# The shared expert's product and the router's logits in one, and a new order of the projection's tiles, in an encoder layer

## What is computed

```python
x = ln_affine(DN_ALPHA * x + gate1 * mixer(u, p), p['ln1_g'], p['ln1_b'])
u = ln_plain(x) * (1.0 + scale2) + shift2
# moe(u): router and shared expert
scores = jax.nn.sigmoid((xt @ p['w_router']).astype(jnp.float32))      # 1024 x 64
g, up = jnp.split(xt @ p['w_sh_in'], 2, axis=-1)                       # 1024 x 512
shared = (jax.nn.silu(g) * up) @ p['w_sh_out']                         # 256 x 1024
```

## Time and profile before

| what | us |
|---|---|
| time, median of 3 runs (2921.95 to 2924.55) | 2923.84 |
| the profiled execution's own time | 2924.61 |
| its span | 2922.4 |
| TensorE busy | 2761.5 |
| VectorE busy | 1585.7 |
| ScalarE busy | 691.7 |
| GpSimd busy | 1107.5 |
| the tile loop, from the first projection to the experts' first product | 983.7 to 1477.4 |

### The profile page before, as it was taken

One profiled execution on the slowest core, in us unless ns is written; L12 is line 12 of the kernel. 1 busy time (PEld: TensorE's weight loads), 2 busy tenths in 40 slices (PEclk: granted clock), 3 DMA queues, 4 the chain that ended last, 5 costly groups with the idle time before them and its releaser, 6 DMA issues. The chain is left out here.

```text
span 2922.4 us, 31454 instructions
## 1 busy us (share of the span) xinstructions
PE 2761.5 (94%) x9161; PEld 1327.1 (45%) x9161; DVE 1585.7 (54%) x2552; ACT 691.7 (24%) x1205; POOL 1107.5 (38%) x1150
## 2 busy tenths in 40 slices
PE   6999999899999899899899999999999999999990
PEld 2345445455555355444444444444444444444440
DVE  3477257778877477778734333333333333343436
ACT  2354354366666211111100000000000000000004
POOL 2002001100000123233356656666665666565664
PEclk9999999999999899999899999999999999999995
DMA  8531000300000311221187798986978788899647
GB/s 335 190 113 55 18 33 8 154 20 8 12 12 8 141 50 59 87 80 58 58 276 230 222 324 227 314 254 163 291 211 262 205 233 251 273 289 301 184 100 273
DMA packets 189009, 466.46 MB, mean 160 GB/s; under 512 B 21756, under 2 KB 46526, under 8 KB 187518
## 3 DMA queue, kind: packets, MB, share of 16 engines
q1 hardware_dynamic: 137246, 311.89, 29.7%
q0 software_dynamic: 51680, 153.50, 21.6%
HBM read 361.38 MB, written 99.75 MB: 158 GB/s over the span
## 5 line engine op out<-in xcount | busy, mean ns | idle before, releaser
L1249 PE MATMUL mx_pH<-ring,mx_wsi 128*128 (+1 forms) x2096 | 944.3, 593 | 5.0 <-DVE mx_wsi L1171 3.0
L1103 POOL DMA_INDIRECT kT<-s_u,ex_gidx x532 | 602.9, 1133 | 163.8 <-issue 159.0
L1249 PEld LDWEIGHTS mx_pH<-ring,mx_wsi 128*128 128x128 f32 x2096 | 388.5, 190 | 445.3 <-issue 445.2
L1269 PE MATMUL mx_pU<-qT,mx_hT 128*128 x1040 | 467.5, 592 | 0.0
L1171 DVE STREAM_TRANSPOSE mx_wsi<-kT 128x1024 f32<-128x1024 f32 x132 | 164.0, 1242 | 321.1 <-DMA kT<-s_u,ex_gidx 315.3
L1269 PEld LDWEIGHTS mx_pU<-qT,mx_hT 128*128 128x128 f32 x1040 | 197.6, 190 | 248.7 <-issue 248.7
L1127 POOL DMA_INDIRECT s_acc<-mx_wso,ex_sidx x130 | 211.8, 1629 | 187.6 <-DVE mx_wso L1201 125.2
L1201 DVE SCALAR_TENSOR_TENSOR mx_wso<-mx_pU,mx_wsi 128x1024 f32<-128x1024 f32 x130 | 166.8, 1283 | 191.7 <-PE mx_pU L1269 186.7
L1154 ACT ACTIVATE mx_hT<-mx_pB 128x256 f32<-128x256 f32 x130 | 49.8, 383 | 870.1 <-PE mx_pB L1236 870.1
L1175 DVE TENSOR_TENSOR mx_h<-mx_silu,mx_pH 128x256 f32<-128x256 f32 x131 | 54.9, 419 | 330.4 <-ACT mx_silu L1143 329.7
L638 PE MATMUL fr_pF<-fr_uT,fr_wf 128*128 128x512 f32 x512 | 224.9, 595 | 1.3 <-ACT fr_uT L332 1.3
(11 more groups left out here) (311 smaller groups left out, 3169.0 us busy)
## 6 DMA issues: line engine op xcount, KB each, us to landing
ring<-in_w_exp_in SPq DMA_DIRECT2D x64, 2048.0 KB, 11.9
qT<-in_w_exp_out SPq DMA_DIRECT2D x64, 1024.0 KB, 15.5
fr_wq<-in_w_ada SPq DMA_DIRECT2D x32, 512.0 KB, 4.8
kT<-s_u,ex_gidx POOLq DMA_INDIRECT x536
fr_wf<-in_w_in SPq DMA_DIRECT2D x16, 512.0 KB, 5.6
s_u<-v SPq DMA_DIRECT2D x16, 512.0 KB, 2.7
out_z<-s_acc SPq DMA_DIRECT2D x16, 512.0 KB, 11.9
y<-out_z SPq DMA_DIRECT2D x16, 512.0 KB, 4.6
```

The costliest lines, as they stand in the source:

```text
L1103: nc.gpsimd.indirect_dma_start(xg[:, u, g, :], None, u2_q, bass.IndirectOffsetOnAxis(ap=gidx[:, u, g:g + 1].bitcast(U32), axis=0)).then_in ...
L1249: m = nc.tensor.matmul(pH[:], xT[:, u, k, :], wi[:, bass.ds(slot, 1), k, :].rearrange("p a f -> p (a f)"), start=(k == 0), stop=(k == KD - 1))
L1269: m = nc.tensor.matmul(pY[:, h, :], hT[:, c, :], wo[:, bass.ds(slot, 1), c, h * 512:(h + 1) * 512].rearrange("p a d -> p (a d)"), start=(c ...
```

## The change

Three things. The router's weights lie in the same buffer as the shared expert's first weights, ahead of them, and for tiles 1 to 12 the first matmul takes 320 columns (64 logits and 256 for silu) into pH and a second one the other 256 into pB. TensorE's order in a tile becomes: attention half 0, turn, attention half 1, product of 320, product of 256, lru half 0 of the next tile, `gated`, lru half 1 of the next tile, `shared_out`, `rank`. On VectorE the gate stands between the second statistics and their aggregation, and the adding of the shared output goes from `norms(i-1)` to the head of tile i; SyncE stores z and loads x accordingly. New waits: the product of 256 waits for the gate before (h_ready) and for the slots two tiles back, `gated` also for the scores (ez_ready), `rank` also for the gate.

```diff
-        wr, wsi, wso = sb("mx_wr", [P, KD, N_EXP]), sb("mx_wsi", [P, KD, 2 * D_E]), ...
+        wsi, wso = sb("mx_wsi", [P, KD, 2 * D_E + N_EXP]), sb("mx_wso", [P, NB, D_E // P, D])
-        LOG, RNK = 0, 64
+        UP, LOG, RNK = 0, D_E, D_E + N_EXP
+        FIRST = N_EXP + D_E
 # SyncE, tile i
-                if 0 < i <= LATE:
-                    store_z(i - 1)
+                if 2 <= i <= LATE + 1:
+                    store_z(i - 2)
+                if i >= 2 and i + 1 < NT:
+                    load_x(i + 1)
                 sp.wait_ge(u2_ready, i + 1)
...
-                if i and i + 2 < NT:
-                    load_x(i + 2)
 # ScalarE
-                if i > 1:
-                    act.wait_ge(log_mm, i - 1)
+                if 1 < i <= LATE + 1:
+                    act.wait_ge(up_mm, i - 1)
+                elif i > 1:
+                    act.wait_ge(log_mm, i - 1 - LATE)
...
+                scores(i, pB[:, LOG:LOG + N_EXP])
+                if i <= LATE:
                     gated_rows(i)
-                scores(i, pB[:, LOG:LOG + N_EXP])
 # VectorE: in stats, in norms, in gate, in the loop
                 passed(dve, apart)
+                if amid is not None:
+                    gate(amid)
...
-                stats(z, 1, EPS, V2, var2)
+                stats(z, 1, EPS, V2, var2, i - 1 if 0 < i <= LATE else None)
...
-                if 0 < i <= LATE:
-                    add_shared(i - 1)
                 dve.wait_ge(rstd2, i + 1)
...
+                up = bank_of(i + 1)[:, D_E:2 * D_E]
+                if i < LATE:
+                    dve.wait_ge(up_mm, i + 1)
+                    up = pB[:, UP:UP + D_E]
...
             for i in range(NT):
+                if 1 < i <= LATE + 1:
+                    add_shared(i - 2)
                 add_lru(i)
...
-                if 0 < i <= LATE:
-                    gate(i - 1)
                 add_att(i)
 # TensorE
+            def lru_half(i, h):
+                if i and h == 0:
+                    pe.wait_ge(l_added, i)
+                if i == KT and h == 0:
+                    pe.wait_ge(wo_folded, GQ)
+                m = project(pL, 1, lruT, i, h)
+                if h:
+                    m.then_inc(pl_mm, 1)
...
+                if i <= LATE:
+                    for k in range(KD):
+                        m = nc.tensor.matmul(pH[:, 0:FIRST], uT(i, k), wsi[:, k, 0:FIRST], start=(k == 0), stop=(k == KD - 1))
+                    m.then_inc(h_mm, 1)
+
+                    if i > 1:
+                        pe.wait_ge(h_ready, i - 1)
+                    if i > 2:
+                        pe.wait_ge(slots_ready, i - 2)
+                    for k in range(KD):
+                        m = nc.tensor.matmul(pB[:, UP:UP + D_E], uT(i, k), wsi[:, k, FIRST:], start=(k == 0), stop=(k == KD - 1))
+                    m.then_inc(up_mm, 1)
+                    return
...
                 pe.wait_ge(m_ready, i)
                 pe.wait_ge(ez_ready, read)
+                pe.wait_ge(h_ready, min(read, LATE))
...
                 project(pA, 0, attT, i, 0)
+                if i:
+                    turn(i)
+                project(pA, 0, attT, i, 1).then_inc(pa_mm, 1)
                 if i:
                     pe.wait_ge(ut_copied, i)
                 if 0 < i <= LATE:
                     shared_in(i)
-                project(pA, 0, attT, i, 1).then_inc(pa_mm, 1)
+                    lru_half(i + 1, 0)
+                    gated(i)
+                    lru_half(i + 1, 1)
+                    shared_out(i)
...
                 if i >= 2:
                     rank(i - 1, i)
+                if (i == 0 or i > LATE) and i + 1 < NT:
+                    lru_half(i + 1, 0)
+                    lru_half(i + 1, 1)
```

More of the change, by code:

```diff
@@ L1294, in mixing @@
         sem = lambda n: ctx.enter_context(nc.semaphore("mx_" + n))
-        wr, wsi, wso = sb("mx_wr", [P, KD, N_EXP]), sb("mx_wsi", [P, KD, 2 * D_E]), sb("mx_wso", [P, NB, D_E // P, D])
+        wsi, wso = sb("mx_wsi", [P, KD, 2 * D_E + N_EXP]), sb("mx_wso", [P, NB, D_E // P, D])
         rb, ln, iota, tokf = sb("mx_rb", [P, N_EXP]), sb("mx_ln", [P, 2, D]), sb("mx_iota", [P, N_EXP]), sb("mx_tokf", [P, 1])
@@ L1358, in mixing @@
             [sem("u2_stored0"), sem("u2_stored1")])
-        ut_mm, ut_copied, h_mm, silu_ready, h_ready, ht_mm, ht_copied = (sem("ut_mm"), sem("ut_copied"), sem("h_mm"), sem("silu_ready"), sem("h_ready"),
+        up_mm, ut_mm, ut_copied, h_mm, silu_ready, h_ready, ht_mm, ht_copied = (sem("up_mm"), sem("ut_mm"), sem("ut_copied"), sem("h_mm"), sem("silu_ready"), sem("h_ready"),
                                                                         sem("ht_mm"), sem("ht_copied"))
@@ L1393, in _ @@
             load_x(1)
-            sp.dma_start(wsi[:], w_sh_in.rearrange("(k p) f -> p k f", p=P)).then_inc(w_in, 16)
+            sp.dma_start(wsi[:, :, N_EXP:], w_sh_in.rearrange("(k p) f -> p k f", p=P)).then_inc(w_in, 16)
             gate2 = lambda b: mod_d[b:b + 1, 5 * D:6 * D].partition_broadcast(P)
@@ L1398, in _ @@
             sp.dma_start(g2[:], gate2(0)).then_inc(g2_in, 16)
-            for dst, src in ((wr[:], w_router), (rb[:], router_bias.partition_broadcast(P)), (iota[:], iota_d.partition_broadcast(P))):
+            for dst, src in ((wsi[:, :, 0:N_EXP], w_router), (rb[:], router_bias.partition_broadcast(P)), (iota[:], iota_d.partition_broadcast(P))):
                 sp.dma_start(dst, src).then_inc(r_in, 16)
@@ L1504, in silu @@
                     act.wait_ge(h_ready, i - 1)
-                nc.scalar.activation(silu_of(i), bank_of(i)[:, 0:D_E], ACT.Silu).then_inc(silu_ready, 1)
+                nc.scalar.activation(silu_of(i), bank_of(i)[:, N_EXP:FIRST] if i <= LATE else bank_of(i)[:, 0:D_E], ACT.Silu).then_inc(silu_ready, 1)
             def gated_rows(i):
@@ L1513, in scores @@
             def scores(i, logits):
-                act.wait_ge(log_mm, i)
+                if i <= LATE:
+                    act.wait_ge(h_mm, i)
+                    logits = pH[:, 0:N_EXP]
+                else:
+                    act.wait_ge(log_mm, i - LATE)
                 if i > 2:
@@ L1577, in fold, with stats @@
                 nc.vector.scalar_tensor_tensor(wo[:, w, j, :], stg[:, c % 2, :], cg[:, w, j:j + 1], grow[:], ALU.mult, ALU.mult).then_inc(wo_folded, 1)
-            def stats(z, which, eps, var_col, done):
+            def stats(z, which, eps, var_col, done, amid=None):
                 for c in range(2):
@@ L1607, in gate @@
                 dve.wait_ge(silu_ready, i + 1)
-                nc.vector.tensor_tensor(gated_of(i + 1), silu_of(i + 1), bank_of(i + 1)[:, D_E:2 * D_E], ALU.mult).then_inc(h_ready, 1)
+                up = bank_of(i + 1)[:, D_E:2 * D_E]
+                if i < LATE:
+                    dve.wait_ge(up_mm, i + 1)
+                    up = pB[:, UP:UP + D_E]
+                nc.vector.tensor_tensor(gated_of(i + 1), silu_of(i + 1), up, ALU.mult).then_inc(h_ready, 1)
             def router(i):
@@ L1764, in shared_in @@
                     pe.wait_ge(r_in, 48)
+                if i <= LATE:
+                    for k in range(KD):
[9 more added lines that the diff above has]
+                    return
                 for k in range(k0, k1):
-                    m = nc.tensor.matmul(bank_of(i), uT(i, k), wsi[:, k, :], start=(k == 0), stop=(k == KD - 1))
+                    m = nc.tensor.matmul(bank_of(i), uT(i, k), wsi[:, k, N_EXP:], start=(k == 0), stop=(k == KD - 1))
                 if k1 == KD:
@@ L1771, in gated @@
                 pe.wait_ge(h_ready, i)
+                if i <= LATE:
+                    pe.wait_ge(ez_ready, i)
                 for c in range(FC):
@@ L1777, in logits @@
                 for k in range(KD):
-                    m = nc.tensor.matmul(out, uT(i, k), wr[:, k, :], start=(k == 0), stop=(k == KD - 1))
+                    m = nc.tensor.matmul(out, uT(i, k), wsi[:, k, 0:N_EXP], start=(k == 0), stop=(k == KD - 1))
                 m.then_inc(log_mm, 1)
@@ L1805, in block_experts @@
                 nc.tensor.transpose(pB[0:2, LOG:LOG + P], wk[:, 0:2], ident).then_inc(blocks_mm, 1)
+            lru_half(0, 0)
+            lru_half(0, 1)
             for i in range(NT):
                 if i:
[L1809 to L1815, removed]
                     pe.wait_ge(a_added, i)
@@ L1823, in _ @@
                     shared_in(i)
-                project(pA, 0, attT, i, 1).then_inc(pa_mm, 1)
-                if 0 < i <= LATE:
+                    lru_half(i + 1, 0)
                     gated(i)
[L1827 to L1831, removed]
+                    lru_half(i + 1, 1)
+                    shared_out(i)
+                elif i:
+                    if i == LATE + 1:
+                        pe.wait_ge(h_ready, LATE)
+                    pe.wait_ge(ez_ready, i - 1)
+                    pe.wait_ge(slots_ready, i - 2)
                     logits(i, pB[:, LOG:LOG + N_EXP])
-                if 0 < i <= LATE:
-                    shared_out(i)
```

(3 more changed lines are left out.)

## The result

| | before | after |
|---|---|---|
| time, median, us | 2923.77 (2921.95 to 2924.55) | 3016.7 (3015.53 to 3017.7) |
| span of the profiled execution, us | 2922.4 | 3014.3 |
| TensorE busy, us | 2761.5 | 2774.1 |
| start of turn 1, 2, 3, us | 1011.76, 1041.30, 1068.66 | 1012.85, 1038.93, 1073.66 |
| start of turn 13 and 16, us | 1355.62, 1422.92 | 1452.15, 1515.93 |

The ratio is 1.0319, with a 95% interval of 1.0304 to 1.0333: 93 us slower. The loss lies between turn 2 and turn 13: 1355.62 - 1041.30 = 314.3 us before, 1452.15 - 1038.93 = 413.2 after, 98.9 more. Outside it the changed kernel gains 3.5 us from turn 1 to 2 and 3.5 from turn 13 to 16, and begins 1.1 later.

What follows compares the result with a forecast made beforehand. Ordinary tiles were taken as bound by TensorE without waits; the change would close a ring of 35.1 us plus 2.6 of clock per step, adding 94.3 us to 2923.84: 3018 us, 8 in 10 between 2992 and 3038.

Steps and rivals of the forecast that it cites:

- The products: TensorE's 320- and 256-column products take 4.31 and 3.45 us, so its work falls by 0.83 us in each of 12 tiles.
- Rival 2: The ring closes and narrow products do not hide weight loads, 3.5 us per tile: 3057, or 3033 us; chance 0.07.
- The ring: Turn (eight transposes of u), TensorE's tile through rank sums, `ranks`, `router`, `add_shared`, next turn: a closed chain of 35.1 us.
- the answers: Two semaphore responses between TensorE and VectorE within each step, put at 0.2 us in sum.
- The stall: TensorE idles 8.6 us per step just before the turn, until VectorE's `add_shared` releases it.
- Which wait is last: The turn waits last for `add_shared`, queued behind `ranks`, which waits for the rank sums; other chains are not later.
- Rival 3: VectorE reaches `add_shared` early enough, the ring stays open and TensorE remains the bound at 26.53 us: 2911 us; chance 0.05.
- rival 4: The ring opens in some tiles, so about half the steps are long: about 2965 us; chance 0.06.
- The clock: TensorE's clock falls after each stall before the turn, costing 2.6 us per step, between 1.6 and 3.5.
- the granted clock that I named as a sign: In the profile after, granted clock would be near 0.93 in the stretches from turn to turn, tiles 3 to 12.
- Rival 1: The ring closes but TensorE's clock does not fall, or returns at once: 2995 us; chance 0.12.
- Tile 7 and the ends: Step with weight folds 41.5 us; turn 1 to 2 26.1; turn 13 to 16, paced by VectorE, 63.4.

Runs made afterwards that it cites:

- the filler: Changed kernel with attention half 0 computed three times over ahead of the turn, tiles 3 to 13: 2991.74 us.
- the run with both cuts: Changed kernel with rank sums behind attention half 1 and the addition of the shared output between `ranks` and `router`: 2909.72 us.
- the run with more in the ring: Changed kernel plus two VectorE statistics instructions between `router` and the addition, tiles 2 to 12: 3026.53 us; between norms and `ranks` instead: 3016.61 us.
- the first two experiments: Changed kernel, either with VectorE's addition put ahead of `ranks`: 2932.16 us; or with TensorE's rank sums moved just behind attention half 1: 2929.44 us.

## Why the prediction was right, step by step

- **The products**: computed 4.31 and 3.45 us from a line through the rows of 128 and 512 columns; measured 4.31 and 3.45. At 256 columns an instruction costs 3.45 / 16 = 0.216 us, so its weight load stays hidden. Rival 2 is out.
- **The ring**: computed 35.1 us; 34.73 at the one step at full clock before the turn that ends it, 35.05 with the filler. Its pieces, computed and measured: from the turn to the rank sums' end 23.25 and 23.14 (turn 2, at full clock); `ranks` and `router` 10.41 and 10.42 (1136.70 to 1147.12); the addition 1.22 and 1.22; the answers 0.2 in sum, measured 0.03 and 0.10. The stall was set at 8.6 and is 8.3.
- **Which wait is last**: shown by cutting the ring at each joint (2932 and 2929 us) and by the same two instructions inside and beside it (3026.5 and 3016.6). Rival 3 was what the changed kernel would be without the ring; the run with both cuts gives 2909.7, where rival 3 had 2911. No step from turn 3 to turn 13 is below 37.3 us, so rival 4, a ring open in some tiles, is out too. VectorE's 21 us per tile were as before all along; its busy share said nothing of the order.
- **The clock**: 2.6 us per step was taken; measured are 37.45 - 35.05 = 2.4 in the tile shown, and 2.3 to 2.8 over the nine ordinary steps. The rows of the instructions give the same: 1.74 - 0.87 for the turn and 5.06 - 3.44 for the half, 2.5 us. The value held, the way to it only in part. I took granted clock below full, times the length of the stretch, as loss. In the changed kernel that gives 0.14 x 37.45 = 5.2 us, twice the real loss, because the clock also stands low while TensorE waits, where it costs nothing: granted clock is 0.69 over the 8.33 us of waiting (1140.15 to 1148.48), which is 2.6 of the 5.2. In the two stretches around tile 7 of the kernel before, the same product came near the truth: TensorE's busy time there is 3.6 and 1.9 us above the ordinary 27.36, against 3.5 and 1.6 by the product. For the same reason the granted clock that I named as a sign, near 0.93, was 0.86. That stalls of 8.3 us would cost what stalls of up to 4.6 us had cost was assumed, not shown; the run with more in the ring has costs from 1.4 to 3.0 us after stalls of one length. So the nearness of 2.6 is partly luck. Rival 1 is out.
- **Tile 7 and the ends**: the fold's step was put at 41.5 us and is 40.34; turn 13 to 16 was 63.4 and is 63.8; turn 1 to 2 26.1 and 26.08. Turn 16 comes 93.0 us later than before, against 94.3 predicted.

The measured 3016.7 lies 1.3 us below the 3018 predicted. The pieces were off by about as much each, and partly cancel: turn 1 came 1.1 us later than taken and turn 2 to 3 was 0.4 shorter, the nine ordinary steps were 1.2 shorter in sum, the fold's step 1.2 shorter, and turn 13 to 16 0.4 longer.

## What to carry to other kernels

Sum up the work of each engine, but then follow every buffer from its reader to its next writer through all queues: an instruction that frees a buffer must not stand behind a wait for the writer's own last work. Where such a ring is closed, its length is the step, whatever the busy shares; it opens by moving either the release ahead of the wait or the awaited work earlier in its queue, and best so that both have something to spare. A saving on the bound engine shows only as far as the next chain has slack. In the old order VectorE's way to the next turn had 0.7 us to spare, and the matmuls taken away, 1.73 us of logits, were part of what covered it: nothing was gained. With both joints opened an ordinary step is 0.8 us shorter, and turn 1 to turn 16 takes 397.6 us instead of 411.2, which includes about 3 us in the first step, most of it clock, and 3 in the last three.

## What the runs showed of the hardware that was not expected

- Added matmuls made the kernel faster: 6.9 us more of them per tile in a wait of 8.3 us brought 25 us in all, since the clock did not fall. (The prediction does not speak of it; the expectation of that run did.)
- The time at the low level after a stall is not the same for each, not even after stalls of one length: after 8.33 us of waiting the turn and the half behind it took 6.85 us, after 9.66 us of waiting 5.71, and after 9.70 us 7.31, against 4.31 at full clock.
- Waits of 1.6 to 1.9 us in the ordinary tiles, as in the first two experiments, left the granted clock at 1.00. In the first of them one wait of 2.12 us was followed by 1.7 us of loss, and one of 2.50 us, in tile 7, by none (the lru half behind it is 3.60 us long, as at full clock): the length of a short wait alone did not decide it.
- VectorE keeps its order while it waits, which the prediction did count on. The Trainium skill, "TensorE: Matmul & The Clock Gate", section "Architectural detail: the array is 16× 32×32, not 1× 128×128", states that its queue is strictly first in, first out; the traces agree: the addition never ran before `router`, though its input was there over 10 us earlier (the shared output's matmuls end by 1136.28, the addition starts at 1147.16).
